# Output projection by seven half-block products, in a hybrid attention and convolution layer

## What is computed

```python
merged = jax.nn.sigmoid(g_mix_a) * y_attn + jax.nn.sigmoid(g_mix_b) * y_conv
sub = gate * (merged @ w_out[layer] + b_out[layer])
x = _layer_norm(DEEPNORM_ALPHA * x + sub, ln_g[layer], ln_b[layer])
```

## Time and profile before

| | |
|---|---|
| median of 3 runs | 1870.26 us (1868.84 to 1872.65) |
| profiled execution | 1868.47 us, its span 1866.7 us |
| PE busy | 1849.8 us, 99% of the span |
| DVE busy | 1214.1 us, 65% |
| ACT busy | 840.7 us, 45% |
| POOL busy | 183.0 us, 10% |

### The profile page before, as it was taken

How to read it: one execution, slowest core, us unless ns; L and a number is a source line. 1 busy time by engine, 2 the same in 40 slices (tenths; PEclk the granted TensorE clock), 3 DMA queues, 4 the chain that set the end, 5 groups by cost and what they waited for, 6 DMA issues and landing times.

```text
span 1866.7 us, 24546 instructions
## 1 busy us (share of the span) xinstructions
PE 1849.8 (99%) x8879; PEld 1508.0 (81%) x8879; DVE 1214.1 (65%) x2086; ACT 840.7 (45%) x1493; POOL 183.0 (10%) x305
## 2 busy tenths in 40 slices
PE   8999999999999999999999999999999999999998
PEld 7788888888888888878878888888888888888886
DVE  8755744456666666675686766666657576646776
ACT  5644633445545555666674545555454310012221
POOL 0223011100000000111210000000111100000000
PEclk9999999999999999999999999999999999999999
DMA  9866523332322222455853222222354988784442
GB/s 372 296 234 242 200 111 113 98 128 72 111 88 95 86 95 82 153 190 180 296 212 101 94 80 91 82 88 87 113 176 135 287 238 225 219 276 135 147 136 101
DMA packets 156648, 292.38 MB, mean 157 GB/s; under 512 B 35344, under 2 KB 87312, under 8 KB 152816
## 3 DMA queue, kind: packets, MB, share of 16 engines
q1 hardware_dynamic: 131056, 202.87, 33.9%
q0 software_dynamic: 25184, 87.35, 12.7%
q10 hardware_dynamic: 288, 0.59, 0.1%
HBM read 202.37 MB, written 88.38 MB: 156 GB/s over the span
## 4 chain that ended last, share of the span: by engine, by line
PE 95%; DVE 2%; ACT 1%; DMA 1%; issue 1%; ACTq 0%; POOL 0%; DVEq 0%
PE acc L1120 22%; PE acc L1125 21%; PE acc L1128 21%; PE acc L1329 3%; PE acc L1278 3%; PE acc L1282 3%; PE acc L1321 3%; PE acc L1325 3%; PE acc L1274 3%; PE score L1185 2%; PE xb L1218 2%; PE acc L1136 1%; PE xb L1201 1%; PE pt_o L1201 1%; DMA vt_d<-room 1%
## 5 line engine op out<-in xcount | busy, mean ns | idle before, releaser
L1120 PE MATMUL acc<-t_hi,w_hi 128*128 128x512 f32 x1848 | 509.2, 397 | 3.0 <-DVE room L1625 1.8
L1125 PE MATMUL acc<-t_lo,w_hi 128*128 128x512 f32 x1848 | 495.0, 390 | 0.0
L1128 PE MATMUL acc<-t_hi,w_lo 128*128 128x512 f32 x1848 | 494.9, 390 | 0.0
L1125 PEld LDWEIGHTS acc<-t_lo,w_hi 128*128 128x128 f32 x1848 | 346.9, 188 | 74.1
L1128 PEld LDWEIGHTS acc<-t_hi,w_lo 128*128 128x128 f32 x1848 | 346.9, 188 | 73.8
L1120 PEld LDWEIGHTS acc<-t_hi,w_hi 128*128 128x128 f32 x1848 | 337.1, 188 | 82.2 <-issue 13.1
L1625 DVE TENSOR_TENSOR room<-acc,part 128x512 f32<-128x512 f32 x198 | 136.8, 691 | 219.7 <-PE acc L1128 213.9
L1421 ACT ACTIVATE part<-acc,cols 128x512 f32<-128x512 f32 x198 | 136.8, 691 | 209.8 <-PE acc L1128 209.4
L1625 DVE TENSOR_TENSOR room<-room 128x512 f32<-128x512 f32 (+3 forms) x223 | 176.5, 795 | 73.8 <-ACT room L1451 30.7
L1625 DVE TENSOR_TENSOR w_lo<-w_raw,w_hi 128x512 fp32r<-128x512 f32 x272 | 183.7, 687 | 40.8 <-ACT w_hi L1404 39.2
L1404 ACT CAST w_hi<-w_raw 128x512 fp32r<-128x512 f32 x264 | 162.8, 617 | 90.2 <-PE acc L1128 87.6
...
...
## 6 DMA issues: line engine op xcount, KB each, us to landing
w_raw<-in_w_tiles SPq DMA_DIRECT2D x132, 512.0 KB, 4.5
gate_d<-room POOLq DMA_DIRECT2D x64, 256.0 KB, 3.8
w_raw<-gate_d SPq DMA_DIRECT2D x32, 512.0 KB, 5.6
qk_d<-room POOLq DMA_DIRECT2D x24, 512.0 KB, 5.1
...
conv_d<-room POOLq DMA_DIRECT2D x16, 512.0 KB, 3.0
mix_d<-w_raw POOLq DMA_DIRECT2D x32, 256.0 KB, 5.6
```

Of the source, the lines that this page charges most:

```text
L1120: nc.tensor.matmul(to, w_hi[:, s, k], t_hi[:, p, k], start=(first and k == 0), stop=False, skip_group_check=True)
L1125: nc.tensor.matmul(to, w_hi[:, s, k], t_lo[:, p, k], start=False, stop=False, skip_group_check=True)
L1128: mm = nc.tensor.matmul(to, w_lo[:, s, k], t_hi[:, p, k], start=False, stop=(last and k == KH - 1), skip_group_check=True)
```

## The change

The output projection becomes Strassen-Winograd too. The 2048 tokens are 8 blocks (`NO`) of 256 tokens. The merged rows of a block are the stationary side (two tiles of 128 tokens by two halves of the 1024 inner rows) and the scaled w_out the moving side (two halves of inner rows by two of 512 columns). A block takes seven calls of `product`, numbered NS to NALL-1, 84 matmuls where two tiles took 96. With it come these parts:

- The sums of w_out's quarters: four times during the input projection (`WQ_AT`) SP loads a part of `wos_d` (`load_wq`), DVE makes four subtractions (`sum_wq`) and POOL stores 1 MB to `to_d`. During units 24 to 31 and just behind them SP loads the seven 1 MB operands (`load_to`), ACT rounds (`round_to`) and DVE splits them (`split_to`).
- The merged rows are loaded by `load_m` into the raw weight buffer, two DMAs of 512 KB a block, and go through `combine`, `round_w` and `split_w` as weights do. For this, gates and sums of units 24 to 31 move to other buffers (`gates_of`, `merged`); `load_merge` of units 27 to 31 now waits until the sum three units earlier is stored.
- gate·b_out is one row, written to DRAM by POOL (`gb_d`) in unit 25, after DVE formed it there from two loads (`gb`, `xs[0]`).
- The residual: ACT multiplies a tile of x by alpha (`scale_x`), then POOL issues a DMA that adds the row `gb_d` to it in SBUF, 512 KB a tile (`residual`).
- DVE adds each product's PSUM bank into x in place (`take_y`, seven a block; four of them also sum the row), ACT takes the squares (`deviation`), and DVE centers and scales a tile in two instructions of 1024 columns (`center`), the second of which applies the scale and ln_b together.

```diff
 def product(n):
+   if n in (NS, NS + 1, NS + 3, NS + NP):
+       pe.wait_ge(conv_gated, M0 + 4 + {NS: 1, NS + 1: 3, NS + 3: 4, NS + NP: 2}[n])
...
-for tt in range(NTT):
...
-            for k in range(KT):
-                mm = nc.tensor.matmul(to, m_l[:, k], wo_hi[:, k, w], start=False, stop=(k == KT - 1))
+for n in range(NS, NALL):
+    product(n)
 # POOL
 for n in range(NMU):
     store_m(n)
+    if n == M0 + 1:
+        pool.wait_ge(gb_ready, 1)
+        pool.dma_start(gb_d, gb[0:1, :]).then_inc(gb_out, 16)
+        pool.wait_ge(gb_out, 16)
+residual(0)
+residual(1)
+for h in range(NO):
+    if h < NO - 1:
+        residual(2 * h + 2)
+        residual(2 * h + 3)
+    shift_row(2 * h)
+    if h < NO - 1:
+        shift_row(2 * h + 1)
+def residual(tt):
+    pool.wait_ge(x_scaled, tt + 1)
+    if tt >= 4:
+        pool.wait_ge(r_taken, 2 * (tt // 2) - 2)
+    pool.dma_start(xs[tt % NX], gb_rows, accum_op=ALU.add).then_inc(r_in[tt // 2 % 2], 16)
+def load_to(p):
+    sp.wait_ge(mc_done, M0 + (0, 2, 4, 6, 8, 8, 8)[p])
...
+                    for p, when in ((1, 3), (2, 4), (3, 6)):
+                        if n == M0 + when:
+                            load_to(p)
+                    if n == M0 + 5:
+                        load_x(0)
+                load_to(4)
+                load_to(5)
+                load_to(6)
 # DVE
+def take_y(n):
+    dve.wait_ge(prod, n + 1)
+    if first is None:
+        dve.wait_ge(r_in[tt // 2 % 2], 32 * (tt // 4 + 1))
...
+def center(tt):
+    dve.wait_ge(std_ready, tt + 1)
...
+for m in range(NS, NALL + 1):
+    if m > NS:
+        take_y(m - 1)
+    h, p = (m - NS) // NP, (m - NS) % NP
+    if p == 0 and h:
+        center(2 * h - 2)
+    if p == 1 and h:
+        center(2 * h - 1)
+    for n, when in enumerate((-4, -3, -2, 0)):
+        if (m - when) % NP == 0 and NG + (when < 0) <= (m - when) // NP < NG + NO:
+            combine((m - when) // NP, n)
+    if m + 3 < NALL:
+        split_w(m + 3)
+    if NS < m <= NS + 3:
+        split_to(m - NS + 3)
+finish_last()
```

More of the change, by code:

```diff
@@ L159 @@
 LAST = NTT - 1
+NO = NTT // 2
+NALL = NS + NO * NP
+NX = 6
+WQ_AT = [ATT_END + 4 + 6 * r for r in range(KH)]
+M0 = NMU - KT
 def blocks_of(j):
@@ L208, in build @@
     wos_d = dram("wos_d", (KT, P, D))
+    to_d = dram("to_d", (4, P, KH, CH))
+    gb_d = dram("gb_d", (1, D))
+    gb_rows = gb_d.broadcast_to([P, D])
     stat_d = dram("stat_d", (2, NPAIR * 2 * NBLK, P))
@@ L910, in _ @@
+                load_to(6)
+                sp.wait_ge(gb_ready, 1)
+                sp.wait_ge(ya_done, NMU)
+                for to, src in ((g_bc, ln_g), (b_bc, ln_b)):
+                    sp.dma_start(to, src.broadcast_to([P, D])).then_inc(bc_in, 16)
+                load_x(1)
+                load_x(2)
+                for h in range(2, NO):
+                    load_m(h)
+                    if h >= 3:
+                        load_x(h)
                 for half in range(2):
-                    sp.wait_ge(affine, LAST + half + 1)
+                    sp.wait_ge(last_affine, half + 1)
@@ L1116, in product @@
                         pe.wait_ge(c22_out, g + 1)
-                    to, s = bank(g, p), n % RING
+                    to = bank(g, p)
+                    hi_w, lo_w, hi_t, lo_t = w_slot(hi_parts, n), w_slot(lo_parts, n), t_part(hi_parts, n), t_part(lo_parts, n)
                     first, last = p in (0, 1, 3), p in (6, 5, 3)
                     for k in range(KH):
-                        nc.tensor.matmul(to, w_hi[:, s, k], t_hi[:, p, k], start=(first and k == 0), stop=False,
+                        nc.tensor.matmul(to, hi_w[:, k], hi_t[:, k], start=(first and k == 0), stop=False,
                                          skip_group_check=True)
@@ new lines, in center @@
+                def center(tt):
+                    r = tt % 2
+                    dve.wait_ge(std_ready, tt + 1)
+                    if tt >= 2:
+                        dve.wait_ge(normed, tt - 1)
+                    own_t.up(nc.vector.reciprocal(rstd[:, r:r + 1], std[:, r:r + 1]))
+                    if tt < 2:
+                        dve.wait_ge(bc_in, 64)
+                    dve.wait_ge(nmu_ready, tt + 1)
+                    own_t.wait()
+                    nc.vector.scalar_tensor_tensor(out=xs[tt % NX], in0=xs[tt % NX], scalar=nmu[:, r:r + 1], in1=g_bc,
+                                                   op0=ALU.add, op1=ALU.mult).then_inc(centered, 1)
+                    dve.wait_ge(centered, tt + 1)
+                    nc.vector.scalar_tensor_tensor(out=xs[tt % NX], in0=xs[tt % NX], scalar=rstd[:, r:r + 1], in1=b_bc,
+                                                   op0=ALU.mult, op1=ALU.add).then_inc(normed, 1)
@@ new lines, in finish_last @@
+                def finish_last():
+                    y, r = xs[LAST % NX], LAST % 2
+                    dve.wait_ge(var_ready, 1)
+                    for half in range(2):
+                        o = slice(half * CH, (half + 1) * CH)
+                        own_t.up(nc.vector.scalar_tensor_tensor(out=y[:, o], in0=y[:, o], scalar=mv[:, 0:1], in1=g_bc[:, o],
+                                                                op0=ALU.subtract, op1=ALU.mult))
+                        if half == 0:
+                            dve.wait_ge(std_ready, LAST + 1)
+                            own_t.up(nc.vector.reciprocal(rstd[:, r:r + 1], std[:, r:r + 1]))
+                        own_t.wait()
+                        nc.vector.scalar_tensor_tensor(out=y[:, o], in0=y[:, o], scalar=rstd[:, r:r + 1], in1=b_bc[:, o],
+                                                       op0=ALU.mult, op1=ALU.add).then_inc(last_affine, 1)
```

409 lines of the change are left out of this document (222 added, 187 removed).

## The result

| | |
|---|---|
| median of 5 runs | 1878.11 us (1875.82 to 1882.34) |
| kernel before, 5 runs | 1870.26 us (1868.84 to 1872.65) |
| ratio after / before | 1.0044, 95% interval 1.0027 to 1.0062 |
| profiled execution | 1877.03 us, its span 1875.2 us |

The kernel became slower by 0.44%, some 8 us; the prediction was 5.8 us faster. One of the six executions of e10 took 10512 us and is left out of its median in the table of the experiments. The page of the changed kernel has these lines where the earlier trace rows stand for the kernel before: the head, busy times, and the chain by engine.

The account below looks back on a forecast made before the run. The prediction took PE alone to bound the output projection. Its terms, -21.7 + 2.1 + 11.1 + 2.7 = -5.8 us, gave 1864.5 us against the median of 1870.26, range 1857 to 1877.

Parts of the forecast that it names:

- Term 1: PE's work in the output projection: 672 matmuls instead of 768, -21.7 us if PE never waits.
- Term 3: Start of the output projection: block 0 waits for its first two accumulating DMAs, +11.1 us.
- R: Moment when both accumulating DMAs of block 0 have landed, taken as 1699 us.
- Link (b): Units 25 to 31, before the projection: w_out operand 3 lands at 1682, unit 31 is merged at 1688.1 us.
- Link (c): Behind unit 31's merge: POOL issues store and two accumulates until 1689.7; the pair, between single and double cost, lands at 1699.
- Early: Rival, start of the projection: the accumulate pair lands by 1694, net -10.9 us, 1859.4 us; chance 0.2.
- Slow in every block: Rival, projection blocks: accumulates land so late that they set the block's period, net +14.0 us at 16 us; chance 0.15.
- DVE sets the blocks: Rival, projection blocks: centers cost 0.5 us more or DVE waits for ACT's deviation, net +1 to +2, 1872 us; chance 0.12.
- far from 7 to 10 us: Sign at the projection's start: the prediction is wrong if the accumulate's landing, shown directly, is far from 7 to 10 us.
- Term 2: DVE's order in a block makes PE wait before product 2: 0.3 us in each of 7 blocks, +2.1 us.
- Term 4: The tail after the last product: one center of tile 14 stands before the last tile's, +2.7 us.
- The sums of w_out: Subtractions during the input projection: hidden, no cost; up to 2 us a group if transfers take 8 us each.

Follow-up runs that it names:

- e10: e7 and e8 together, edits of the changed kernel: 1860.32 us, ratio 0.9942 to the kernel before.
- e6: Changed kernel, with SP's loads behind unit 31 issued only when the first pair of accumulating DMAs has landed: 1877.65 us, ratio 1.0038 to the kernel before.
- e3: Changed kernel, with the 16 residual DMAs copying the row over x instead of adding it: 1874.80 us, ratio 1.0024 to the kernel before.
- e4: Changed kernel, with each block's last sum of merged rows moved on DVE from product 0 to product 1: 1876.87 us, ratio 1.0032 to the kernel before.
- e8: Changed kernel, with the four groups of w_out sums seven products apart instead of six: 1877.45 us, ratio 1.0037 to the kernel before.
- e7: Changed kernel, with DVE adding the first two tiles' row, SP issuing tile 14's store, and e4's later sum: 1860.52 us, ratio 0.9942 to the kernel before.

## Why the prediction was wrong

- **What bounds the kernel, Term 1.** Right: 672 matmuls at 0.2265 us, -22.0 us (the table). No block reaches 19.03 us, because of waits and of what they do to the matmuls behind them.
- **Term 3, the start.** The mechanism was right link by link: PE stands before product 2 of block 0, released by DVE's taking, that by the DMA on `gb_d`, issued behind the merge of unit 31; and block 1 starts at R + 16.3 where R + 16.2 was said. This is the step that failed most: it was mis-sized, +18.0 for +11.1, R at 1706.9 for 1699. (R is 7.9 us late and the term 6.9, since T itself lies 1.1 later.) Two links carry this, in equal parts.
  - Link (b) had operand 3 landed at 1682; it was 1686, so the merge came at 1692.1 and not 1688.1. The step took 6.8 MB to flow from 1663 on. But SP issued one transfer of 1 MB at 1663.01 and then stood until 1670.86; the loads of two gates, operand 2, two tiles of x and operand 3 all left between 1670.86 and 1673.34. The load at 1670.86 waits until the sum of unit 27 is stored; POOL issued this store at 1663.00, and in the trace it lands 7.85 us later. Against a flow of 420 GB/s the rows below lack some 2.2 us until 1670 (288 GB/s) and 1.8 from 1670 to 1672 (50 GB/s at a share of 0.20), and another microsecond until 1674 (205 GB/s). The text had the issue times ("issued only at 1671 to 1673") and still counted from 1663.

```profile
1663.00:1670.00 7.00, 7.00 (x33) 5.79 (x32) 2.38 (x4) 0.00 (x0) 1.08 (x2) 1.00 0.87 288
1670.00:1672.00 2.00, 2.00 (x11) 1.65 (x10) 0.00 (x0) 1.30 (x1) 0.00 (x0) 1.00 0.20 50
1672.00:1686.00 14.00, 14.00 (x64) 11.59 (x63) 8.97 (x9) 3.07 (x4) 1.08 (x2) 1.00 0.86 323
```

  - Link (c) had the pair landed 10.9 us after the merge; it took 14.8. The central value was set between single and double cost. Double cost at half share would have been 13.3, and the measured rates, 223 GB/s against 404, speak for nearly double; so 2.4 of the 3.9 us are this choice. The other 1.5 lie beyond double cost and below the text's upper end, 16.9 ("1705 if the x loads slow them further"). SP does issue four more tiles of x, 2.1 MB, from 1698.79 on, ahead of the landing; that they are the 1.5 us is likely and not shown, since e6 held them back together with all other loads. e3 prices the addition at 4.3 us, e6 all neighbours at 5.7.
  - The clock behind the wait was forecast right: "+0.4 at most", and about 0.4 is what it cost. The length of the wait was not: by the text's own times it would be 9.1 us and not 8.5, and it was 15.9.
- **The rivals on the accumulates.** *Early* is excluded: the pair landed 14.8 us after the merge. The Trainium skill ("DMA: Bandwidth & Descriptors", section "Anatomy of one DMA — SWDGE (gpsimd) path") gives a DMA 2.0 us plus bytes over 436 GB/s, which by its estimate was 4.4 us for the pair. Measured were 7.6 from the second issue with no loads beside it, and 13.3 with them; the fit doesn't hold for these accumulates. The same page's section "Rules for kernel authors" says that an accumulate reads its destination and writes it later, and the 223 GB/s at full DMA share agree with that. *Slow in every block* is excluded too: from block 1 on no taking waits for a row. *DVE sets the blocks* is not what came either: in the seven blocks DVE waits 15.7 us for products. Of the signs, "far from 7 to 10 us" came true for the second accumulate (13.3 us), not for the first (10.1).
- **Term 2, DVE in a block.** Right in place, too small in size. The text's own chain gives 0.2 us (5.6 less 5.44), its term 0.3; the view lists a wait of 0.35. The whole is +5.5 instead of +2.1: in blocks 2 to 7 product 2 starts 0.51 us late and the first matmuls behind the wait cost 0.10 more, 0.62 a block and not 0.3, and in block 1 PE waits 1.3 us for DVE, which had waited 0.84 for ACT's deviation. The second center costs nothing as long as the first place does (e4).
- **Term 4, the tail.** The center cost 2.6 us for 2.7. The drain of POOL, +3.3 us, is a step that is missing from the prediction altogether. The trace of the kernel before shows it, with 7.74 us from 1846.5 on, but hidden, and I had read the tail from DVE alone. The change put POOL's last store 20 us later, at 1866.68, and so uncovered it.
- **The sums of w_out.** The text gave them 0 and named the case of "up to 2 us a group" if transfers slow down. They did, once with an effect: DVE waited 5.25 us and PE 1.0 (PE's waits for DVE ahead of T rose by 0.9; e8 takes them away). By the medians of e8 and e10 this is not shown to cost time.
- **The range.** It held the misses one by one and not together: +4, +4, +3.4, +3.2 and +1 all have one sign. The terms were taken at values at which little else interferes, and most of these errors are of one kind, work put next to other work.

The forecast of a gain of this size was not empty: e7, with the same seven products, is at 1860.5 us. That is with other code at the edges of the stage, so it does not make the forecast right. What failed is the price of the new waits at these edges: 13.8 us (11.1 and 2.7) were forecast and 23.9 (18.0 and 5.9) measured.
